# Eleven expert blocks multiplied in plain fp32 from unsplit weights, and three one-hot buffers in place of five

## The reference

```python
def peer_ffn(xn, w_peer_q, sub_keys, expert_u, expert_v):
    qh = (xt @ w_peer_q).reshape(T, 8, 2, 128)
    s = jnp.einsum('thpd,hpnd->thpn', qh, sub_keys)
    sv, si = lax.top_k(s, 16)                       # per head and half
    ... best, pick = lax.top_k(cand, 16)            # 16 experts of 16384 per head
    gates = jax.nn.softmax(best, axis=-1)
    u = expert_u[ic]                                # ic: the chosen experts
    hval = jnp.einsum('cd,chkd->chk', xc, u)
    a = gc * jax.nn.gelu(hval, approximate=False)
    return jnp.einsum('chk,chkd->cd', a, expert_v[ic])
```

## Time and profile before

| | before |
|---|---|
| time, median of 3 executions | 1320.24 us (1316.26 to 1321.51) |
| time of the profiled execution | 1316.06 us |
| its span, first to last instruction | 1314.2 us |
| TensorE busy (product records) | 1296.9 us, 99% |
| VectorE busy | 1069.0 us, 81% |
| ScalarE busy | 820.9 us, 62% |
| clock granted to TensorE, mean | 0.999 |

### The profile page before, as it was taken

The page is one execution under the profiler, slowest core; times in us unless marked ns, Lnnn a source line. Parts: engine busy times, 40 slices in busy tenths (PEclk is TensorE's granted clock), DMA queues, the critical chain, the costliest instruction groups (busy, mean ns, idle before and its releaser), DMA issues.

```text
span 1314.2 us, 21763 instructions
## 1 busy us (share of the span) xinstructions
PE 1296.9 (99%) x8061; PEld 1198.1 (91%) x8061; DVE 1069.0 (81%) x1974; ACT 820.9 (62%) x1601; POOL 228.8 (17%) x163
## 2 busy tenths in 40 slices
PE   8999999999999999999999999999999999999998
PEld 6998888888889888889999999999999999999996
DVE  6867676666678666778999889999999888898885
ACT  6886555555556555454677789888665555555553
POOL 3002030000000000001000011000334445445520
PEclk9999999999999999999999999999999999999999
DMA  6533365556535344654666565655788999999972
GB/s 231 180 121 136 114 219 190 186 192 193 170 137 182 137 136 169 227 190 168 207 209 220 189 220 203 216 207 200 274 301 318 368 365 342 355 363 362 343 281 90
DMA packets 82784, 292.74 MB, mean 223 GB/s; under 512 B 10397, under 2 KB 11053, under 8 KB 82422
## 3 DMA queue, kind: packets, MB, share of 16 engines
q1 hardware_dynamic: 68182, 239.65, 52.2%
q0 software_dynamic: 14496, 51.69, 10.7%
HBM read 288.95 MB, written 2.34 MB: 222 GB/s over the span
## 4 chain that ended last, share of the span: by engine, by line
PE 85%; DVE 8%; ACT 3%; DMA 2%; issue 2%; POOL 0%; SPq 0%; POOLq 0%; DVEq 0%; ACTq 0%
PE bank L2408 83%; DVE wl L665 3%; DMA raw<-in_wts 2%; DVE rows L1603 1%; PE bank L2506 1%; PE bank L2494 1%; ACT wh L1747 1%; DVE gates L1635 1%; DVE oi L1580 0%; DVE gates L1588 0%; DVE oj L1576 0%; DVE us L1594 0%; ACT kdz L1753 0%; DVE St L855 0%; ACT oi L2328 0%
## 5 line engine op out<-in xcount | busy, mean ns | idle before, releaser
L2408 PE MATMUL bank<-hTb,wh 128*128 128x416 f32 (+3 forms) x2768 | 826.1, 363 | 4.1 <-DVE wl L665 3.4
L2408 PE MATMUL bank<-hTb,wl 128*128 128x208 f32 (+2 forms) x2584 | 651.8, 264 | 0.0
L665 DVE TENSOR_TENSOR wl<-raw,wh 128x1024 fp32r<-128x1024 f32 x429 | 524.3, 1229 | 125.5 <-ACT wh L1747 124.5
L1747 ACT ACTIVATE wh<-raw 128x1024 fp32r<-128x1024 f32 x429 | 449.6, 1056 | 201.4 <-DMA raw<-in_wts 118.7
L2408 PEld LDWEIGHTS bank<-hTb,wh 128*128 128x128 f32 (+1 forms) x2768 | 504.9, 188 | 27.5 <-issue 6.7
L2408 PEld LDWEIGHTS bank<-hTb,wl 128*128 128x128 f32 (+1 forms) x2584 | 491.5, 190 | 4.8
L2408 PE MATMUL bank<-wh,hTb 128*128 128x512 f32 (+2 forms) x552 | 175.0, 398 | 1.5 <-DVE hTb L699 1.5
L2408 PEld LDWEIGHTS bank<-wh,hTb 128*128 128x128 f32 (+1 forms) x552 | 102.2, 187 | 24.4 <-DVE wl L665 1.7
L645 POOL DMA_INDIRECT rows<-in_v_rows,pick x48 | 99.6, 2075 | 99.8 <-DVE acc L1614 85.7
L645 POOL DMA_INDIRECT rows<-in_u_rows,pick x48 | 76.4, 1592 | 229.6 <-DVE dots L1603 226.8
L2408 PE MATMUL bank<-wl,hTb 128*128 128x512 f32 (+2 forms) x276 | 100.3, 389 | 0.0
(11 more groups left out here) (429 smaller groups left out, 1403.7 us busy)
## 6 DMA issues: line engine op xcount, KB each, us to landing
raw<-in_wts SPq DMA_DIRECT2D x441, 512.0 KB
x<-in_x SPq DMA_DIRECT2D x4, 256.0 KB, 6.4
sk<-in_sk SPq DMA_DIRECT2D x1, 1024.0 KB, 7.3
spill<-x SPq DMA_DIRECT2D x1, 1024.0 KB
x<-spill SPq DMA_DIRECT2D x4, 256.0 KB
rows<-in_u_rows,pick POOLq DMA_INDIRECT x48
rows<-in_v_rows,pick POOLq DMA_INDIRECT x48
gb<-in_g_ffn SPq DMA_DIRECT2D x1, 512.0 KB
```

Of the source, the lines that this page charges most:

```text
L665: e.tensor_tensor(b[:, :], raw[u % RAW][:, :], a[:, :].bitcast(F), ALU.subtract).then_inc(S("lo"), 1)
L1747: e.activation(parts_of(u)[0][:, :], raw[u % RAW][:, :], ACT.Copy).then_inc(S("hi"), 1)
L2408: return e.matmul(o, l, r, start=first, stop=last, skip_group_check=True)
```

## The change

Eleven units of U, n = 55, 61, ..., 115 (`WHOLE`), are no longer split. TensorE multiplies `raw` itself with `xt`, which holds the unsplit turned tokens, in plain fp32: 8 products of 208 columns in one bank (`unit_whole`). For these units `high` and `low` do nothing, there is no low half to copy, and `summed` returns; GELU reads the bank. All eleven were units of the kind whose low half VectorE added. The buffer of `raw` is released by the unit's product (`done`) and not by `lo`. VectorE computes `xt = hTh + hTl` once, into the area that held two of the five pairs of one-hot buffers, so NB is 3.

```diff
-NP, NB = 50, 5
+NP, NB = 50, 3
+WHOLE = range(55, 116, 6)
...
-        oj = [M(f"oj{i}", [128, 4, 128]) for i in range(3)] + [sb(f"oj{i}", [128, 4, 128], F, XO + 2048 * (i - 3))
...
+        xt = sb("xt", [128, 8, TN], F, XO)
+        oj = [M(f"oj{i}", [128, 4, 128]) for i in range(3)]
...
+        U0 = nth("U", ORDER[0])
+        whole_units = tuple(U0 + n for n in WHOLE)
+
+        def nth_split(u):
+
+            return u + 1 - sum(w <= u for w in whole_units)
...
         def added(n):
 
-            return n < SUMMED or n < GATED and n % 2 == 0
+            return n not in WHOLE and (n < SUMMED or n < GATED and n % 2 == 0)
...
                 for u in range(loaded[0], n):
                     if u >= RAW:
-                        e.wait_ge(S("lo"), u - RAW + 1)
+                        if u - RAW in whole_units:
+                            e.wait_ge(S("done"), u - RAW + 1)
+                        else:
+                            e.wait_ge(S("lo"), nth_split(u - RAW))
...
             def low(n):
                 for u in range(lows[0], min(n + 1, len(units))):
-                    e.wait_ge(S("hi"), u + 1)
+                    if u in whole_units:
+                        continue
+                    e.wait_ge(S("hi"), nth_split(u))
...
+                if i == 1:
+                    e.wait_ge(S("in_end"), 16)
+                    e.tensor_tensor(xt[:, :, :], hTh[:, :, 0:TN].bitcast(F), hTl[:, :, 0:TN].bitcast(F),
+                                    ALU.add).then_inc(S("hT_lo"), 1)
...
             def summed(n):
 
+                if n in WHOLE:
+                    return
...
             def block_out(n):
 
                 e.wait_ge(S("done"), nth("U", ORDER[n]) + 1)
-                if not added(n):
-                    e.wait_ge(S("gelu"), n - 1)
-                copy((low_half if added(n) else us)[n % 2][:, :], B[2 + n % 4][:, TN:2 * TN]).then_inc(S("u_out"), 1)
+                if n not in WHOLE:
+                    if not added(n):
+                        e.wait_ge(S("gelu"), n - 1)
+                    copy((low_half if added(n) else us)[n % 2][:, :], B[2 + n % 4][:, TN:2 * TN]).then_inc(S("u_out"), 1)
                 high(nth("U", ORDER[n]) + LOOK)
...
+            def unit_whole(unit, bank):
+
+                n = nth(*unit)
+                assert n == started[0], (unit, units[started[0]])
+                started[0] += 1
+                e.wait_ge(S(f"raw{n % RAW}"), 16 * (n // RAW + 1))
+                e.wait_ge(S("hT_lo"), 25)
+                for k in range(8):
+                    t = mm(bank[:, 0:TN], raw[n % RAW][:, two(128, k)], xt[:, k, :], k == 0, k == 7)
+                t.then_inc(S("done"), 1)
...
-                unit_M(("U", ORDER[n]), B[2 + n % 4], width=TN)
+                if n in WHOLE:
+                    unit_whole(("U", ORDER[n]), B[2 + n % 4])
+                else:
+                    unit_M(("U", ORDER[n]), B[2 + n % 4], width=TN)
```

More of the change, by code:

```diff
@@ L295, in program @@
         M = Area(R0, RE)
-        oj = [M(f"oj{i}", [128, 4, 128]) for i in range(3)] + [sb(f"oj{i}", [128, 4, 128], F, XO + 2048 * (i - 3))
-                                                              for i in (3, 4)]
-        oi = [sb("oi0", [128, 4, 128], F, X0 + 3072)] + [M(f"oi{i}", [128, 4, 128]) for i in (1, 2)] + \
-             [sb(f"oi{i}", [128, 4, 128], F, XO + 2048 * (i - 1)) for i in (3, 4)]
+        xt = sb("xt", [128, 8, TN], F, XO)
+        oj = [M(f"oj{i}", [128, 4, 128]) for i in range(3)]
+        oi = [sb("oi0", [128, 4, 128], F, X0 + 3072)] + [M(f"oi{i}", [128, 4, 128]) for i in (1, 2)]
         GT0 = M.p
@@ L351, in program, with split_of @@
         Q0 = nth("T", "w_peer_q_2", 0, 512, 0)
+        U0 = nth("U", ORDER[0])
+        whole_units = tuple(U0 + n for n in WHOLE)
+        def nth_split(u):
+            return u + 1 - sum(w <= u for w in whole_units)
+        def split_of(n):
+            return min(n, NE - 1) + 1 - sum(w <= n for w in WHOLE)
         def parts_of(u):
@@ L389, in nth_sum @@
                 return n - 3
-            return 13 + n - nth_added(n)
+            return 12 + split_of(n) + max(0, n - NE + 1) - nth_added(n)
         def added(n):
-            return n < SUMMED or n < GATED and n % 2 == 0
+            return n not in WHOLE and (n < SUMMED or n < GATED and n % 2 == 0)
         def nth_added(n):
@@ L400, in nth_out @@
         def nth_out(n):
-            return 13 + n
+            return 12 + split_of(n) + max(0, n - NE + 1)
         def of_expert(n):
@@ L2268, in gelu @@
                     e.wait_ge(S("u_add"), nth_added(n))
-                else:
+                elif n not in WHOLE:
                     e.wait_ge(S("u_sum"), nth_sum("U", n))
@@ L2413, in begin @@
                 started[0] += 1
-                e.wait_ge(S("lo"), n + 1)
+                e.wait_ge(S("lo"), nth_split(n))
                 return parts_of(n)
```

## The result

The changed kernel took 1322.38 us, the median of 11 executions (1320.21 to 1326.3), beside 1317.9 us for the kernel before on the same chip (11 executions). It is the same by the bound of 0.5% and lies in the range, but the sign is the other one. The profiled execution has a span of 1318.4 us and took 1320.21 us, 4.2 us more than the one of before.

What follows compares the result with a forecast made beforehand. TensorE, 99% busy, was taken to bound the kernel, losing 8.0 us to a late VectorE. Products +4.6, given back 8.0, of which 1.9 stay: -1.5 us from 1320.24, so 1318.7 us, range 1314.8 to 1324.5.

Steps and rivals of the forecast that it cites:

- TensorE, +0.42 us a unit, 4.6 in all: Units 51 to 127 of U: a whole unit's 16 records take 2.82 us against 2.40 split; eleven cost 4.6 us.
- Given back beside the gates, 3.0 us: Beside the gates: a relieved VectorE is no longer late, so TensorE's 3.0 us of excess vanish.
- NB = 3 at nothing: One-hot buffers: three pairs make no wait, since the buffers' previous product has ended; cost nothing.
- xt at nothing: VectorE near 605 us: the sum of about 2.0 us is hidden in VectorE's waits for ScalarE, so costs nothing.
- these waits take it up: VectorE's waits for ScalarE of 1.28 us before 610.96 and 1.36 us before 621.49 absorb xt's 2.0 us.
- the uncovered case: VectorE near 605 us: if its waits did not absorb xt, the sum would cost up to 2.0 us.
- Late loads, 1.2 us: Behind units 103, 109, 115: load of n + 4 waits for unit n's last product; 0.4 us each, bounds 0 and 8.
- the rival of late loads: Behind the gates: landings of 7 us cost 2.9 us at each of three units, giving 1326.2 us; chance 0.13.
- Given back behind the gates, 5.0 less 0.7 us: Behind the gates: 4.5 us of lag and 0.5 us at V's first product come back, except 0.7 us after unit 115.
- The forecast's lower end: Whole sum at its best: 4.4 us added, 8.5 given back, -4.1 us, giving 1316.1 us.
- That the extra products show and the stalls stay: Units 51 to 127: +4.6 us, only 0 to 3 given back, 1321.8 to 1324.8 us; chance 0.12.
- Plain fp32 at half rate: TensorE's whole units: an fp32 product takes only twice its columns' time, 1.39 us a unit, giving 1301 us; chance 0.02.

Runs made afterwards that it cites:

- the copied versions: Changed kernel with xt at the gates and ScalarE copying whole units' raw as plain fp32, freeing buffers early: eleven units 0.9985, four 0.9984, six behind the gates 0.9976.
- the eleven: Changed kernel with xt at the gates and all eleven whole units copied by ScalarE: 1316.05 us, 0.9985; with loads held instead, 1320.58 us, 1.0016.
- the six: Changed kernel with xt at the gates and only six whole units, 103 to 123, copied by ScalarE: 1315.32 us, 0.9976; with loads held instead, 1.0009.
- the added wait alone: Kernel before, all units split, but loads into the buffers of units 55, 61 to 115 wait for the unit's last product: 1321.22 us, ratio 1.0032.
- eight copied units: Changed kernel with xt at the gates and only the eight whole units beside the gates (55 to 97), raws copied by ScalarE: ratio 1.0006.

## Why the prediction failed, step by step

**TensorE, +0.42 us a unit, 4.6 in all: right.** The record of 208 columns takes the 0.176 us that the line through 128 and 256 columns gave. The distances between the last products of units show 0.43 us a unit beside the gates (3.73 us with its one-hots, where a split unit takes 3.30) and 0.44 behind them (2.84 for 2.40). There is no start-up at the change of types.

**Given back beside the gates, 3.0 us: right.** From unit 54 to 102 the eight whole units cost 3.4 us and the time grew by 0.62, so 2.8 came back; the ratios agree with 1.0006 against 1.0003, though their intervals would allow 2 us either way. The excess of the last six units over early ones was 0.33 us in place of 1.01.

**NB = 3 at nothing: right.**

**xt at nothing: wrong, 1.8 us.** The step that failed was "these waits take it up". A wait of VectorE for ScalarE absorbs work only if ScalarE's own release does not depend on what VectorE delays. Here VectorE's late `qh` held TensorE, TensorE held ScalarE, and the wait came 1.8 us later with its full length. The prediction kept the right price, 2.0 us, as the uncovered case, and gave it no place in the sum. The row that would have told is what stands behind `xt` in VectorE's queue, the sum of the query block, and TensorE's key scores that start at once when it ends.

**Late loads, 1.2 us: the mechanism right, the size wrong, up to 4.1 to 4.3 us.** The prediction worked out when a landing is late and then took 0.4 us for each exposed unit without a row for that size; this is the other step that failed. Its working was short in two places. From landing to `wl` it had 3.0 us; the trace has 3.3 us at unit 113, with TensorE's product 0.14 us behind, so that a landing up to some 3.8 us is free and not 4.2, and the two that counted took 4.94 and 4.23 us. And it looked at the load of n + 4 alone. The load of n + 5, held behind it, landed 5.8 us after its issue and met a turn of VectorE with gathered rows in it: 4.5 us from landing to TensorE, and a wait of 1.0 us. That is the rival of late loads, whose price of 2.4 to 2.9 us was set for a landing of 6.6 to 7.1 us a unit; measured, against the copied versions, are 1.4 us a unit with the eleven (4.1 / 3) and 0.7 with the six (4.3 / 6), each with an uncertainty of some 2 us in the sum, and with the gain of the early start in it. Beside the gates nothing that shows was lost, as forecast. Why, is in part argued: VectorE has been relieved there, and the added wait alone, in the kernel with nothing relieved, cost 2.8 us in G.

**Given back behind the gates, 5.0 less 0.7 us: not seen with held loads, and possible in size once the loads are free.** From eight copied units to eleven copied ones the ratio falls from 1.0006 to 0.9985, 2.8 us less, where 3 x 0.42 - 4.3 = -3.0 was forecast. The intervals leave between 0.4 and 5 us for it, and the early start of the loads is in it too. With held loads the step from eight units to eleven goes the other way, from 1.0006 to 1.0016.

The sum with the two measured terms in place: -1.5 + 1.8 (`xt`) + 2.9 (4.1 for 1.2) = +3.2 us, beside 3.8 measured [2.2, 5.3]. The 4.1 us are an upper bound for their term, for the reason given, so this agreement is no proof of the sum. The forecast's lower end had 8.5 us given back, more than the 8.0 that it called all there is to give.

*The rivals.* That the extra products show and the stalls stay gives the measured time (+1.6 to +4.6 us by 1321.8 to 1324.8, measured +3.8), but only half for its reason: the stalls beside the gates went, and behind the gates there are as many again, 3.4 us of waits for 2.8. Plain fp32 at half rate is out, and with it the rule of an output rate halved, if it is meant for a whole product, by 0.176 us for 208 columns, four columns' time a product.

*What stays open.* How much of the gain of the copies is the earlier start of the loads: a kernel with no whole unit whose loads leave as early, or one with copies whose loads wait for the turn in which `wl` would be made, was not run. Why eleven units cost as much with held loads as six more densely placed ones, and how the loss is shared between the stretch behind the gates and the start of V, is below what these runs resolve. So is the order of the copied versions: 0.9976, 0.9984 and 0.9985 overlap.

## What to carry to other kernels

A wait in the profile is spare time only for work whose delay does not reach the engine that ends the wait; follow the loop (VectorE to TensorE to ScalarE and back) before putting work into it. Where a ring's buffer is released later, price every load that stands behind in the queue, from its issue through its landing to the consumer, with the work that stands in the way there, and ask whether a cheap copy can free the buffer instead: here ScalarE, with time to spare, took 4 us back, in part by freeing it earlier than before. And put relief where the relieved engine is late; beside the gates eight of the eleven units cost 3.4 us and gave 2.8.

## What the runs showed of the hardware

Three loads of 512 KB that are issued within 1.2 us of each other landed after 3.2, 5.8 and 6.3 us, after 4.9, 5.8 and 6.6 us and after 4.2, 5.2 and 6.1 us: the first of a group lands soonest. In the kernel before, with the loads further apart, those of the same stretch took 3.1 to 7.1 us, so a landing of 6 us alone does not mark a group.

A sum of two fp32 tiles in SBUF on GpSimd, 1664 columns in 3.79 us, made a VectorE subtraction of two fp32 operands last 5.38 us in place of 1.22. The Trainium skill (SBUF — State Buffer, Who interferes with whom) says that a VectorE instruction with two SBUF inputs contends with a GpSimd instruction that reads SBUF, that the port pair they share is an exclusive lock, and that the order of issue decides who blocks. The trace agrees with the lock, since the subtraction ended 1.09 us after GpSimd did. The recorded start of VectorE is 0.50 us ahead of GpSimd's, and it was still the one that waited; the profile does not show the order of issue, and its spans on GpSimd are rough, so this decides nothing about the order.
